# The in-projection of an encoder: norm finished before the first products, token loads issued earlier, output kinds interleaved

## What is computed

```
h = rmsnorm(x, attn_norm[j])                 # x * rsqrt(mean(x*x) + eps) * g
proj = h @ w_in                              # 1024 -> 4096
q, k, v, z = jnp.split(proj, 4, axis=-1)
...
o = o.reshape(B, S, D) * jax.nn.silu(z)
```

## Time and profile before

| | |
|---|---|
| median of 3 runs | 2998.72 us (2998.64 to 3003.08) |
| the profiled execution | 3001.8 us |
| its span in the trace | 2999.7 us |
| mean granted TensorE clock, share of full speed | 0.974 |
| PE busy, share of the span | 2834.2 us, 94% |
| DVE, ACT, POOL busy | 1831.8, 1740.7, 1637.9 us |
| end of the in-projection in the trace | about 801 us |

### The profile page before, as it was taken

One profiled execution on the slowest core, in us unless ns is written; L12 is line 12 of the kernel. 1 busy time (PEld: TensorE's weight loads), 2 busy tenths in 40 slices (PEclk: granted clock), 3 DMA queues, 4 the chain that ended last, 5 costly groups with the idle time before them and its releaser, 6 DMA issues. The chain is left out here.

```text
span 2999.7 us, 41691 instructions
## 1 busy us (share of the span) xinstructions
PE 2834.2 (94%) x15098; PEld 2493.8 (83%) x15098; DVE 1831.8 (61%) x2402; ACT 1740.7 (58%) x3126; POOL 1637.9 (55%) x1060
## 2 busy tenths in 40 slices
PE   3899999999899999999999999998999899899898
PEld 3899999999778787878888888886688899887687
DVE  7668767866476777777777777776886200441322
ACT  4777766776477777777777777775443321322321
POOL 5888764654266566656665666665664320230642
PEclk8999999999999999999999999999999999999899
DMA  2654464356344413141313232121565522555752
GB/s 84 197 173 166 146 198 127 118 181 201 101 130 138 107 34 102 35 108 36 98 46 76 65 74 64 37 90 60 199 207 172 187 90 77 158 168 186 263 186 102
DMA packets 281816, 374.03 MB, mean 125 GB/s; under 512 B 22923, under 2 KB 258507, under 8 KB 276140
## 3 DMA queue, kind: packets, MB, share of 16 engines
q1 hardware_dynamic: 279404, 369.14, 39.6%
q10 hardware_dynamic: 2080, 2.10, 0.2%
q0 software_dynamic: 128, 0.13, 0.0%
HBM read 258.04 MB, written 125.97 MB: 128 GB/s over the span
## 5 line engine op out<-in xcount | busy, mean ns | idle before, releaser
L1296 DVE TENSOR_REDUCE pa_half_max<-pa_score 128x1 f32<-128x1024 f32 x512 | 624.2, 1219 | 324.9 <-PE pa_score L1066 324.4
L1220 ACT ACTIVATE pa_p<-pa_score,pa_neg_max 128x1024 f32<-128x1024 f32 x512 | 567.7, 1111 | 68.6 <-DVE pa_neg_max L1302 68.4
L206 PE MATMUL ia_acc<-ia_xh,ia_wh 128*128 128x384 f32 x1344 | 459.9, 342 | 73.3 <-DVE ia_xl L686 44.1
L1122 PE MATMUL pa_o_acc<-pa_wt,pa_vv 128*128 128x256 f32 x2048 | 514.0, 380 | 1.5 <-ACT pa_o_out_s L1259 1.5
L1062 PE MATMUL pa_score<-pa_ka,pa_qa 128*128 128x512 f32 x1024 | 454.9, 444 | 13.2 <-ACT pa_p L1220 6.6
L207 PE MATMUL ia_acc<-ia_xl,ia_wh 128*128 128x384 f32 x1344 | 456.2, 339 | 0.0
L208 PE MATMUL ia_acc<-ia_xh,ia_wl 128*128 128x384 f32 x1344 | 455.8, 339 | 0.0
L1198 ACT ACTIVATE pa_wt<-pa_turned 128x512 f32<-128x512 f32 x512 | 306.3, 598 | 241.4 <-PE pa_turned L1096 236.4
L443 POOL TENSOR_TENSOR ia_w_sums<-ia_raw 128x512 f32<-128x512 f32 x240 | 334.3, 1401 | 174.3 <-PE ia_acc L208 158.8
L1066 PE MATMUL pa_score<-pa_kb,pa_qb 96*128 96x512 f32 x1024 | 422.9, 413 | 0.0
L1122 PEld LDWEIGHTS pa_o_acc<-pa_wt,pa_vv 128*128 128x128 f32 x2048 | 366.2, 190 | 44.8 <-ACT pa_o_out_s L1259 3.2
(11 more groups left out here) (284 smaller groups left out, 5338.5 us busy)
## 6 DMA issues: line engine op xcount, KB each, us to landing
ia_raw<-attn_w_in SPq DMA_DIRECT2D x46, 1024.0 KB, 6.1
qk_hi<-ia_hi SPq DMA_DIRECT2D x96, 192.0 KB, 3.1
qk_lo<-ia_c SPq DMA_DIRECT2D x96, 192.0 KB, 2.8
pa_ka<-qk_hi SPq DMA_DIRECT2D x32, 512.0 KB, 8.9
fl_slices<-normed SPq DMA_DIRECT2D x26, 512.0 KB, 6.5
ia_h<-x_cols SPq DMA_DIRECT2D x24, 384.0 KB, 5.6
v<-ia_c SPq DMA_DIRECT2D x48, 192.0 KB, 5.5
attn_gate<-ia_c SPq DMA_DIRECT2D x48, 192.0 KB, 1.9
```

The costliest lines, as they stand in the source:

```text
L206: pe.matmul(out, a_hi(k), b_hi(k), start=first and n == 0, stop=False)
L1122: mm = pe.matmul(acc, vv[:, k], wt[:, g % 2, k], start=k == 0, stop=k == NB - 1)
L1220: act.activation(dst[:, half * HALF:(half + 1) * HALF], score[:, (4 * q + j) % RING].rearrange("p a b -> p (a b)"), ACT.Exp, bias=neg_max[ ...
L1296: dve.tensor_reduce(half_max[:, q % 2, n, half:half + 1], score[:, (4 * q + j) % RING].rearrange("p a b -> p (a b)"), AX_X, ALU.max).then_ ...
```

## The change

Three edits, all in `project_quads`.

1. The first span is normalised before its products. ACT squares the eight units into three buffers in turn, TensorE sums each unit over the partitions as soon as it is squared (`sum_first_squares`, two matmuls with the matrix of ones for a unit, into one bank for each half), ACT takes the root and DVE the reciprocal, and `weigh` multiplies with norm weight and `rstd` as in the other spans. `scale` and its waits are gone. The first two weight pairs are loaded by SP, the first after four token units.
2. The tokens of the next span are asked for at pair j = 0 to 7, between the second and the third tile's store, ahead of the weights; they were asked for at j = 1 to 8 ahead of the first store.
3. The order of the pairs alternates: split, plain, split, plain, ... in the first eight, split, silu, ... in the last eight (`turn_of`).

```diff
-        pairs = [(kind, dest, 2 * j) for n, kind, dest in sections for j in range(n // 2)]
+        listed = [(kind, dest, 2 * j) for n, kind, dest in sections for j in range(n // 2)]
+        halves = [x for j in range(SPLITS // 2) for x in (j, j + SPLITS // 2)]
+        turn_of = [x for j in range(SPLITS) for x in (halves[j], SPLITS + j)]
+        pairs = [listed[x] for x in turn_of]
...
-        places = []
+        places = [("squares", 0, 0), ("squares", 0, 1)]
...
         def wait_tile(eng, n, k):
-            if n < W_PAIRS:
-                eng.wait_ge(scaled, 4 * n + k + 1)
-            else:
-                eng.wait_ge(fused, FUSED * n + DONE[k])
+            eng.wait_ge(fused, FUSED * n + DONE[k])
+
+        def square_of(e):
+            return (squares[:, 0], squares[:, 1], square[:])[e % 3]
...
                 for n in range(QUADS):
                     p, j = divmod(n, W_PAIRS)
-                    if p + 1 < SPANS and 1 <= j < 9:
-                        load_unit(p + 1, j - 1)
...
                     store(n, C21)
                     store(n, C12)
+                    if p + 1 < SPANS and j < 8:
+                        load_unit(p + 1, j)
                     load_weights(n + 3)
...
-                def scale(n, k):
-                    if n < W_PAIRS:
-                        half = 1 if k in (C12, C22) else 0
-                        pool.wait_ge(inverted, half + 1)
-                        pool.wait_ge(fused, FUSED * n + DONE[k])
-                        pool.tensor_tensor(tile(n, k), tile(n, k), rstd[:, 0, half], ALU.mult).then_inc(scaled, 1)
...
+                def sum_first_squares(e):
+                    pe.wait_ge(squared, e + 1)
+                    for b in range(2):
+                        mm = pe.matmul(bank_of(("squares", 0, e // 4)), ones[:], square_of(e)[:, b], start=e % 4 == 0 and b == 0,
+                                       stop=e % 4 == 3 and b == 1)
+                    mm.then_inc(square_read, 1)
...
+                for e in range(8):
+                    sum_first_squares(e)
...
-                        if p:
-                            x = dve.scalar_tensor_tensor(out=h[:, k, half], in0=h[:, k, half], scalar=norm_w[:, k:k + 1],
-                                                         in1=rstd[:, p % 2, half], op0=ALU.mult, op1=ALU.mult)
-                        else:
-                            x = dve.tensor_scalar(h[:, k, half], h[:, k, half], norm_w[:, k:k + 1], None, ALU.mult)
+                        x = dve.scalar_tensor_tensor(out=h[:, k, half], in0=h[:, k, half], scalar=norm_w[:, k:k + 1],
+                                                     in1=rstd[:, p % 2, half], op0=ALU.mult, op1=ALU.mult)
```

More of the change, by code:

```diff
@@ L403, in store, with load_first @@
                     sp.dma_start(dest[1][b, :, t0:t0 + COLS], tile(n, k)).then_inc(stored[n % 2], 16)
-                for e in range(8):
+                def load_first(u):
+                    sp.dma_start(raw[:, u], w_dram[0].rearrange("(k p) n -> p k n", p=P)[:, :, turn_of[u] * 2 * P:(turn_of[u] + 1) * 2 * P]).then_inc(raw_in[u], 16)
+                for e in range(4):
                     load_unit(0, e)
@@ L408, in _ @@
                         sp.dma_start(norm_w[:], norm_dram).then_inc(consts_in, 16)
+                load_first(0)
+                for e in range(4, 8):
+                    load_unit(0, e)
+                load_first(1)
                 load_weights(2)
@@ L470, in low @@
                         pool.tensor_tensor(tile(n, k).bitcast(F32R), tile(n, k), f32(tile_hi(n, k)), ALU.subtract).then_inc(out_lo_pool, 1)
[L472 to L485, removed]
+                for x in range(8):
+                    weight_sum(x)
                 for slot in range(LAST + 4):
@@ L552, in square_unit @@
                     act.wait_ge(x_in[e], 16 * (p + 1))
-                    wait(act, square_added, 6 * p + 3 * (e // 4) + max(e % 4 - 1, 0))
-                    act.activation(square[:] if e % 4 else squares[:, e // 4], unit(p, e), ACT.Square).then_inc(squared, 1)
+                    if p == 0:
+                        wait(act, square_read, e - 2)
+                        dst = square_of(e)
+                    else:
+                        wait(act, square_added, 6 * (p - 1) + 3 * (e // 4) + max(e % 4 - 1, 0))
+                        dst = square[:] if e % 4 else squares[:, e // 4]
+                    act.activation(dst, unit(p, e), ACT.Square).then_inc(squared, 1)
                 def weight_high(s):
@@ L580, in root @@
                 def root(p, half):
-                    act.wait_ge(square_summed, 2 * p + half + 1)
-                    if p >= 2 and half == 0:
-                        act.wait_ge(scaled, 4 * W_PAIRS)
+                    if p == 0:
+                        act.wait_ge(square_read, 4 * half + 4)
+                    else:
+                        act.wait_ge(square_summed, 2 * (p - 1) + half + 1)
                     act.activation(rstd[:, p % 2, half], bank_of(("squares", p, half)), ACT.Sqrt, bias=eps[:, 0:1], scale=1.0 / D).then_inc(rooted, 1)
@@ L630, in _ @@
                             take(n, M3, C12)
-                    if n == 0 and t in (4, 6):
-                        root(0, (t - 4) // 2)
                     if slot < 4:
@@ L726, in _ @@
                 x_ready_sum(0, 2)
-                for s in range(3, 7):
-                    weight_low(s)
+                for w in range(3, 7):
+                    weight_low(w)
                 for slot in range(LAST + 4):
@@ L734, in _ @@
                             fuse(n, no)
-                        if n == 0 and t in (5, 6):
-                            invert(0, t - 5)
                     if n and t == 0:
```

54 lines of the change are left out of this document (22 added, 32 removed).

## The result

The changed kernel takes 2968.34 us (median of 4 runs, 2963.53 to 2969.55) against 2998.68 for the kernel before (2996.99 to 3003.08, 4 runs): ratio 0.9894, interval 0.9876 to 0.9911. 30.3 us were gained; 18.7 were forecast. The profiled execution took 2963.53 us, its span in the trace 2961.7.

What follows compares the result with a forecast made beforehand. In-projection (first 801 us) loses 101.8 us at the start and in work for the next span, beside which nothing has slack. Terms sum to -18.7: 3001.8 to 2983.1 profiled, median 2980 us; range 2967 to 2994, forecast's own 2975 to 2984.

Steps and rivals of the forecast that it cites:

- rival B: Losses at pairs 9, 16, 25 and 32 feed on earlier lateness; half the rest also goes (-12): 2968 us; chance 0.16.
- tokens sooner: Next span's units go out earlier, removing ACT's waits: -3.8 us in pair 23, -2.1 in 25, -1.0 in 9.
- start up to the third set: Serial chain from first unit: first set at 31, third at 52.4 against 51.4; half of that 1.0 taken, +0.5 us.
- rest of pair 0: Two sums and a wait leave TensorE's path, but low parts are then late with DVE full: -1.5 us.
- pairs 3 to 5: Twelve scales leave POOL, and with them the waits of the finishing steps: -2.9 us.
- pair 23: The longest ACT wait for a unit, 5.4 us in pair 22, is gone or under 1: -3.8 us.
- pair 25: ACT's 3.14 us wait heading the chain to the reciprocal goes, less the preceding split pair's finishing: -2.1 us.
- pair 9: Likewise a shorter unit wait removed and scales gone, split-pair finishing added: -1.0 us.
- pair 16: Scales gone gives -2.3 us; remainders of split pair 14 falling into 15 cost +1.0: -1.3 us.
- pair 32, with 33: No scaling to remove at pair 32; remainders of split pair 30 fall into 31: +1.0 us.
- Rival A: At the start, TensorE's sums stay at the low clock or turns cost more: third set near 58, 2986 us; chance 0.18.
- The third set decides: At the start, the third set (M1) decides, since everything after it follows closely; expected near 52 us.

Runs made afterwards that it cites:

- e9: Kernel before, with only the eighth token unit of each span asked for at its new, earlier place: 2993.36 us, ratio 0.9995.
- e10: Kernel before, with only the first seven token units of each span asked for at the new, earlier place: 2982.05 us, ratio 0.9963.
- e6: Changed kernel, with the first reciprocal of spans 1 and 2 one set later, behind the additions of M4: 2963.65 us, ratio 0.9899.
- e8: Changed kernel, with each unit's two sum matmuls of the first span done twice (values differ): 2978.33 us, ratio 0.9948.
- e7: Changed kernel, with DVE's low part of the third set ahead of four weight remainders at the start: 2970.08 us, ratio 0.9918.
- e1: Kernel before, with only the first span normalised before its products; old token loads and pair order: 2980.82 us, ratio 0.9944.
- e4: Changed kernel, with the pairs back in the old order: 2963.92 us, ratio 0.9892.
- e12: Changed kernel, with old pair order, late first reciprocal of spans 1 and 2, POOL's sums held back and earlier token rounding at the start: 2958.06 us, ratio 0.9883.
- e2: Kernel before, with only the next span's tokens asked for sooner: 2978.7 us, ratio 0.9942.
- e3: Kernel before, with only the alternating order of pairs: 2985.82 us, ratio 0.9962.
- e5: Changed kernel, with the token loads at their old place: 2968.64 us, ratio 0.9914.
- e11: Changed kernel, with POOL's weight sums after the first held until the first half is weighed, and token rounding before the second root: 2965.29 us, ratio 0.9904.

## Why the prediction was wrong in its size

The direction held, and so did the terms read off a single wait; but the changed kernel came out 12 us faster than forecast, outside the forecast's own range (2975 to 2984) and where rival B had it. The step that failed is the term "tokens sooner" for pairs 9 and 25: 3.1 us were forecast and 9.9 measured. In the order of its terms, forecast and measured:

| term | forecast | measured |
|---|---|---|
| start up to the third set | +0.5 | -3.7 |
| rest of pair 0 | -1.5 | -0.3 |
| pair 1 | -7.6 | -7.6 |
| pairs 3 to 5 | -2.9 | -2.9 |
| pair 23 | -3.8 | -3.8 |
| pair 25 | -2.1 | -5.5 |
| pair 9 | -1.0 | -4.4 |
| pair 16 | -1.3 | -2.9 |
| pair 32, with 33 | +1.0 | +1.0 |
| sum | -18.7 | -30.1 |

**Pairs 9 and 25 (6.8 of the 11.4 missing)**: the term "tokens sooner" was mis-sized. It costed the wait that stood at the pair, 3.14 us at the head of the chain of squares, less a price for the split pair's finishing. What these pairs paid for was the lead that ACT's waits for the seven units before had used up: e9 took the last wait away and changed 0.2 and 0.7 us, e10 took the others and got 5.1 and 6.2. The evidence was there: 30.9 us in 13 waits, of which the one at pair 25 was 3.14, the others in pairs that mostly lost nothing themselves. This is rival B's mechanism, losses that feed on earlier lateness. That its 2968 is what came is luck: B had the gain in pairs 16 and 32 too, which gave little or nothing, and took 12 for a half that is about 15 by its own 33 us less the terms already counted; the start and pair 16 made up the rest. The prediction had the last link right, since TensorE did wait for the additions behind the reciprocal. The argument against rival B, that the reciprocal in DVE's order stays, was right for 1.4 us in each (e6) and no more. The finishing that was charged cost 0.7 in each pair (2.7 with the alternation, 2.0 without).

**The start (3.0: 4.2 up to the third set, less 1.2 behind it)**: the two pieces were right, and e8 bears out that the chain is serial, but it was too dear by 3.1 at the first set (28.0 against 31.1): the first unit was there 0.9 us sooner than 5, the eight instructions of the first two units took 4.60 instead of 5.1, warm units 1.45 instead of 1.6, and the second four units began at 17.07 and not at 19. DVE's stretch took 19.9 instead of 21.3 up to the third set. Rival A, the sums held at the low clock, did not come: the third and fourth unit and the last two went at the rate of the high clock, the fifth, behind a pause of 3.48 us, did not (2.93). The rest of pair 0 gave 0.3 instead of 1.5: the sums left TensorE's path, but DVE was busy 16.60 of 16.60 us there. "The third set decides" was wrong (e7), which cost nothing here, because DVE was taken as the bound anyway.

**Pair 16 (1.6)**: this is no more than the spread of that pair. Without the scales and in the old order it gave 3.7 (e1), 2.2 (e4) and 3.8 (e12), with the scales still there 0.2 (e2), so the 2.3 charged to them are not refuted. The scales are also not all of it: the low part of 4.95 ran beside one of POOL's sums of tokens (311.20, 3.48 us) and only then beside a scale, and in the changed kernel, without scales, two low parts there still took 3.10 and 3.99. The charge of 1.0 for the alternation is open too: e3 lost 1.7 more at pair 16, and pair 33 lost 0.8 with the alternation in the changed kernel and e3, but nothing in e5, e7 and e8, which have it as well. The agreement of +1.0 at pair 32 with 33 is within the same spread.

**Right to a few tenths**: pair 1, pairs 3 to 5 and pair 23 (with the doubt that e9 throws on that last loss). Each was read off a wait whose whole cause the change removes. But e1 to e3 show that 3 to 5 and 23 have several removers: any edit that gives ACT or POOL its slack back takes the loss away, or part of it (e1 left 1.7 of the 3.0 in pairs 3 to 5), so the three edits alone give 19.0, 19.0 and 13.1 us of the stage, 51 together, and 30.5 in one kernel (in the medians 14.4, 16.5 and 9.4, 40 together, and 30.3).

## What to carry to other kernels

An engine that takes its work in order pays for a wait later than where it stands. When one waits often for a transfer in pairs that lose nothing, its waits still use up the lead of everything queued behind it; cost the removal of all of them at the next pair without slack, not of the last one. The runs give no rate for it: 28.5 us of such waits between 100 and 775 us went with 11.3 us of loss in pairs 9 and 25. And when several edits free the same lead, count it once: run each alone before adding them, since the cheapest one may do (here either the token loads or the order of the pairs).

## What was not expected of the hardware

In the start, four two-input weighings on DVE took 4.33 us beside POOL's sums of weights and 2.20 with POOL idle, while POOL's five sums took 6.16 us and in e11 four of them took 8.01 beside DVE's two 1536-column operations: either engine can be the one that is slowed, and so the engines do not meet at semaphores alone. A 1536-column low part took 1.76 us alone, 2.51 in e11 and 4.82 in e7 beside POOL. And pair 25 with 2.0 us lost had a granted clock of 1.00, with 7.5 us lost one of 0.84 (e10 and e9).
